# Dealing TensorE's turns anew: fewer visits for value products, levels among the last query slices

## What is computed

```python
def nsa_mixer(h, ...):                      # 16 heads of 64, 4 key/value groups
    q, kc, vc, ks, vs, kw, vw, gl, z = split_cols(h @ w_in, ...)
    q = rope(q); gates = sigmoid(gl)
    v_cmp = compress(vc, pe_v, wv1, wv2)    # silu(flat @ w1) @ w2 over blocks of 32 tokens
    k_cmp = rope(compress(kc, pe_k, wk1, wk2), cmp_end)
    o_c = masked_softmax(q . k_cmp) . v_cmp
    o_s = masked_softmax(q . rope(ks) at the selected blocks) . vs
    o_w = masked_softmax(q . rope(kw) in the window) . vw
    o = gates[0] * o_c + gates[1] * o_s + gates[2] * o_w
    return (o * silu(z)) @ w_out

def hgrn2_mixer(h, ...):                    # 8 heads of 128, chunks of 64
    q_raw, f_raw, i_in, z = split_cols(h @ w_in, ...)
    f = lb + (1 - lb) * sigmoid(f_raw); k = 1 - f; q = silu(q_raw)
    # o[t] = sum over s <= t of (q[t] * k[s] * product of f between) . v[s]
    o = o * rsqrt(mean(o * o) + EPS) * g_norm
    return (o * silu(z)) @ w_out
```

## Time and profile before

| | |
|---|---|
| median of 3 runs | 328.72 us (328.6 to 329.0) |
| profiled execution, first to last instruction (span) | 327.3 us |
| around the span (median less span) | 1.4 us |
| TensorE, matmuls | 316.1 us, 97% |
| TensorE, weight loads beside them | 268.5 us, 82% |
| VectorE | 228.5 us, 70% |
| ScalarE | 188.5 us, 58% |
| GpSimd | 56.8 us, 17% |
| from HBM | 47.97 MB |

### The profile page before, as it was taken

One profiled execution on the slowest core, in us unless ns is written; L12 is line 12 of the kernel. 1 busy time (PEld: TensorE's weight loads), 2 busy tenths in 40 slices (PEclk: granted clock), 3 DMA queues, 4 the chain that ended last, 5 costly groups with the idle time before them and its releaser, 6 DMA issues.

```text
span 327.3 us, 6178 instructions
## 1 busy us (share of the span) xinstructions
PE 316.1 (97%) x2380; PEld 268.5 (82%) x2380; DVE 228.5 (70%) x408; ACT 188.5 (58%) x400; POOL 56.8 (17%) x55
## 2 busy tenths in 40 slices
PE   8999999998999999999999999999999999998993
PEld 5789778867889887777678878999998788897882
DVE  2788953649659978979838716378359988489824
ACT  4694355347686676758545806838355027898223
POOL 0004022070343333446300000100000011111000
PEclk9999999999999999999999999999999999999998
DMA  7999999806390830043260783663663334002011
GB/s 234 393 326 215 272 358 198 258 36 210 97 209 1 194 67 2 0 131 128 75 248 0 259 299 95 240 228 92 212 241 110 150 112 151 3 0 66 0 64 64
DMA packets 28828, 49.41 MB, mean 151 GB/s; under 512 B 3256, under 2 KB 7744, under 8 KB 28800
## 3 DMA queue, kind: packets, MB, share of 16 engines
q1 hardware_dynamic: 25760, 44.30, 43.3%
q10 hardware_dynamic: 2528, 2.69, 4.1%
q0 software_dynamic: 512, 2.03, 1.9%
HBM read 47.97 MB, written 1.05 MB: 150 GB/s over the span
## 4 chain that ended last, share of the span: by engine, by line
PE 63%; DVE 16%; ACT 8%; issue 2%; POOL 2%; ACTq 0%; DVEq 0%; POOLq 0%
PE bank L553 58%; DVE w_lo L1079 6%; ACT w_hi L832 4%; PE bank L732 3%; POOL rp L1442 1%; DVE nmax L1283 1%; ACT prob L952 1%; PE bank L653 1%; DVE qk L1372 1%; DVE ft L1339 1%; DVE qk L1358 1%; DVE prob_t L1295 1%; PE bank L597 1%; DVE zT L1225 1%; DVE zT L1226 0%
## 5 line engine op out<-in xcount | busy, mean ns | idle before, releaser
L1079 DVE TENSOR_TENSOR w_lo<-raw,w_hi 128x1024 fp32r<-128x1024 f32 (+1 forms) x80 | 89.0, 1155 | 34.5 <-ACT w_hi L832 34.3
L553 PE MATMUL bank<-w_hi,h_hi 128*128 128x512 f32 x192 | 77.4, 409 | 2.0 <-DVE h_lo L1182 1.1
L553 PE MATMUL bank<-w_hi,h_lo 128*128 128x512 f32 x192 | 75.1, 391 | 0.0
L553 PE MATMUL bank<-w_lo,h_hi 128*128 128x512 f32 x192 | 75.1, 391 | 0.0
L832 ACT ACTIVATE w_hi<-raw 128x1024 fp32r<-128x1024 f32 (+1 forms) x80 | 72.9, 967 | 2.1 <-issue 1.9
L553 PE MATMUL bank<-h_hi,w_hi 128*128 128x256 f32 x224 | 64.9, 290 | 0.3 <-DVE vc_lo L1261 0.3
L553 PE MATMUL bank<-h_hi,w_lo 128*128 128x256 f32 x224 | 63.4, 283 | 0.0
L553 PE MATMUL bank<-h_lo,w_hi 128*128 128x256 f32 x224 | 63.3, 283 | 0.0
L553 PEld LDWEIGHTS bank<-w_hi,h_hi 128*128 128x128 f32 x192 | 35.9, 188 | 10.6 <-issue 3.7
L553 PEld LDWEIGHTS bank<-h_hi,w_hi 128*128 128x128 f32 x224 | 42.9, 192 | 1.1 <-DVE vc_lo L1261 0.7
L553 PEld LDWEIGHTS bank<-h_lo,w_hi 128*128 128x128 f32 x224 | 42.9, 192 | 0.2
(11 more groups left out here) (199 smaller groups left out, 424.0 us busy)
## 6 DMA issues: line engine op xcount, KB each, us to landing
raw<-in_hg SPq DMA_DIRECT2D x16, 1024.0 KB, 7.4
raw<-in_nsa SPq DMA_DIRECT2D x12, 1024.0 KB, 8.8
raw<-in_nsa_out SPq DMA_DIRECT2D x8, 512.0 KB, 8.5
raw<-in_hg_out SPq DMA_DIRECT2D x4, 1024.0 KB, 6.6
raw<-in_nsa SPq DMA_DIRECT2D x8, 256.0 KB, 5.7
w<-in_w1k SPq DMA_DIRECT2D x2, 1024.0 KB, 16.1
w<-in_w1v ACTq DMA_DIRECT2D x2, 1024.0 KB, 14.6
x_res<-in_x SPq DMA_DIRECT2D x4, 256.0 KB, 5.1
```

What stands on the lines that cost most here:

```text
L553: return nc.tensor.matmul(o, lhsT, rhs, start=start, stop=stop, skip_group_check=True)
L1079: m = V.tensor_tensor(lo, src, hi.bitcast(F32), ALU.subtract)
```

## The change

It replaces the two strings, and with them the numbers that place the splits: SPREAD, GATED_LAG (3 to 4) and LAG. Both strings hold the same letters as before, so that TensorE has the same steps and banks. In ORDER, two H come ahead of the first A. The first x (cmp1 of the keys) stands behind one E and no longer behind four. The g of a roped tile often stand in pairs. The v come in 9 groups and no longer in 13, the groups mixed anew with s, z and t. In H_ORDER, the transposes h and the first V slices change places by one. Three l stand ahead of the last two R. After the last levels the order is z o x o z x z z z z y y, where it was z o z z o z x z x y y, so that o(0,1) comes two slices of z earlier. The four r (V_O0, t1) stand in one run behind the first s, where r and s were mixed to the end.

```diff
--- before.py
+++ after.py
@@ -74,9 +74,9 @@
 LAST_LV = len(LEVELS)
 RECT_LV = (LAST_LV - 2, LAST_LV - 1)
 
-ORDER = 'HAHHBAHHBAHHBABCDCCrCDgDDgEEEEggxFFFGkFIIgJgkKKIgIgKKpxLggpkgppqqkgqzsgqzzgszzgatgzsbsszzztstszzvtcszvvvtstsszvtztsvtzastzsvvttsbstvvvtsosovvcotstssvvttssvttsotvtvvovttovvvvoo'
+ORDER = 'HHHAHHBAAHHBABBCDCrCCggDDggDExEEEFkFFFGgkKIKJggIKIIKxLgqpggppkpqkggqzsgqzgzszgaztgzsbsszzztstzszstvczvvvtsttzssvvatsszztsztvvttsbstvvvvtosstocostssvvsttsvvttsottvvvvottovvvvoo'
 HT_BANKS = ((4, 5, 6, 7), (0, 1, 4, 5))
-H_ORDER = 'aaaabhhbbbcccchdhddeeeefdfFffFFFFFFQFQQQQQQQGGGGGGRRGGRRRRRRllllzzllllzllllzzllllzzllllzllllzllllzzllllzozzozxzxyyoommmmnyynnnrssrsrrs'
+H_ORDER = 'aaaabhbhbbcccchhddeeeeffdfFdfFFFFFFQFQQQQQQQGGGRGGGGGRRRRRlRRlllzzllllzllllzzllllzzllllzllllzllllzlzlllzoxozxzzzyyoommmmnyynnnsrrrrsss'
 CMP_BANKS = ((1, 1, 7), (7, 6, 1))
 ACT_TURNS = (4, 7, 10, 11, 12, 13, 16, 19, 22)
 
@@ -214,11 +214,11 @@
     return kk + 1 if u == 0 else KT + NQ * (u - 1) + kk // 2 + 1
 
 
-SPREAD = {U_KW: (6, 7, 7, 0), U_Q0: (9, 5, 18, 15), U_Q1: (10, 13, 20, 26), U_Z0: (4, 0, 7, 12), U_Z1: (6, 7, 8, 12), U_O0: (17, 14, 28, 45), U_O1: (31, 47, 66, 93), V_V0: (0, 0, 1, 4), V_V1: (0, 0, 3, 6), V_F0: (0, 0, 11, 0), V_Q0: (2, 7, 20, 19), V_F1: (3, 5, 5, 6), V_Q1: (1, 0, 4, 9), V_Z0: (3, 5, 3, 5), V_Z1: (4, 0, 44, 39), V_O0: (0, 3, 2, 2), V_O1: (3, 1, 7, 4)}
-GATED_LAG = 3
+SPREAD = {U_KW: (10, 7, 7, 6), U_Q0: (1, 7, 20, 15), U_Q1: (1, 12, 5, 21), U_Z0: (5, 3, 2, 13), U_Z1: (3, 5, 11, 12), U_O0: (19, 0, 25, 38), U_O1: (31, 57, 78, 96), V_V0: (0, 0, 0, 4), V_V1: (0, 0, 2, 10), V_F0: (2, 0, 8, 0), V_Q0: (2, 0, 23, 25), V_F1: (0, 4, 1, 2), V_Q1: (2, 2, 10, 12), V_Z0: (0, 3, 0, 3), V_Z1: (0, 9, 56, 26), V_O0: (0, 3, 0, 0), V_O1: (0, 3, 7, 6)}
+GATED_LAG = 4
 CMP_LAG = 4
 GATED_AT = [max(LAST[("pv", job)], LAST[Z_GROUPS[-1]] + job) for job in range(4)]
-LAG = {U_O0: 2, U_O1: 3, V_Z0: 1, U_Z0: 1, U_Q1: 1, V_O1: 2, V_Q0: 3, V_F1: 2, V_Z1: 1, V_F0: 2, V_V1: 4, U_Z1: 2, U_KW: 2, U_Q0: 2, V_V0: 1, V_O0: 1, V_Q1: 2}
+LAG = {U_O0: 4, U_O1: 4, V_Z0: 2, U_Z0: 3, U_Q1: 2, V_O1: 2, V_Q0: 3, V_F1: 4, V_Z1: 1, V_F0: 5, V_V1: 4, U_Z1: 2, U_KW: 1, U_Q0: 1, V_V0: 1, V_O0: 4, V_Q1: 2}
 SPLIT_HI_AT, SPLIT_LO_AT = split_places()
```

## The result

| | before | after |
|---|---|---|
| median of the runs | 328.86 us (4 runs: 328.60, 328.72, 329.00 and 619.23) | 333.99 us (332.66 to 335.36, 4 runs) |
| ratio, 95% interval | 1 | 1.0153 (1.0130 to 1.0176) |
| profiled execution, span | 327.3 us | 330.9 us (its time 332.66) |
| mean granted clock of TensorE | 0.996 | 0.984 |

The change makes the kernel slower by 1.5%. Nothing on record explains the one execution of 619.23; without it the median of before is 328.72. The forecast was 329.2 us and its range ended at 331.3. The median is 5.1 us over that of before; the profiled execution is the quickest of the four and accounts for 3.6 of them.

A forecast was written before the change was run, and what follows sets the result against it. TensorE, busy 316.1 of 327.3 us, was taken as the bound. 3.15 - 1.0 - 0.35 + 0 - 1.25 - 0.1 = +0.45 gave span 327.7, with 1.4 around it 329.2 us; range 327.0 to 331.3.

The forecast's parts named there:

- Part 1: Head up to cmp1(0): moved ahead of three E slices, it waits some 5 us for w1k; +3.7 us.
- B: Rival at w1k's load: it lands earlier, at 37.7, making the time 326.8 us; chance 0.20.
- C: Rival at w1k's load: at 389 GB/s it lands at about 31, before TensorE comes; 324.0 us, chance 0.05.
- Part 2: From cmp1(0) to Z0's first slice: three old waits go, -1.8; a new stage 4 bank wait comes, +1.25 us.
- Part 3: Attention: fewer value-product visits -1.07, small pt waits gone -0.45, one new wait for prob_t +0.5; together -1.0 us.
- Rival A: VectorE and ScalarE fall behind in attention, pv visits wait: attention +0.5 instead of -1.0, time 331; chance 0.20.
- Part 4: Second layer's projections and levels: hT pair moved one turn, -0.35 us; the levels taken as 0.
- Part 5: End of HGRN2: o(0,1) earlier, so V_O0's first slice no longer waits for h_lo; -1.25 us.
- 6: Tail: VectorE's last add still starts right with the last matmul; -0.1 us.

The follow-up runs named there:

- filler: Changed kernel with 20 matmuls into an unused bank before the wait for w1k, results unread: 330.64 us, ratio 1.0052.
- second profile: The changed kernel run once more, unaltered, for the spread of its executions: 333.11 us, ratio 1.0138, span 333.6.
- w1k_rows: Changed kernel with w1k in another arrangement, 16 KB pieces instead of 1 KB, still two transfers to 64 partitions each: 331.69 us.
- w1k_2x128: Changed kernel with w1k rearranged as two 1 MB transfers, each to all 128 partitions in 8 KB pieces: 325.92 us, ratio 0.9903.
- w1k_128: Changed kernel with w1k rearranged as one transfer of 16 KB to each of 128 partitions: 326.00 us, ratio 0.9911.
- w1_two: Changed kernel with the second half of w1k issued from ScalarE's queue at about 20.5 us: 331.08 us, ratio 1.0070.
- w1_j: Changed kernel with w1k cut by j into 16 transfers of 128 KB, each to all 128 partitions: 364.39 us, ratio 1.1083.
- att_only: Kernel before with only the new order from Z0's first slice to attention's end, its splits and GATED_LAG 4: 328.69 us, ratio 0.9988.
- h_only: Kernel before with only H_ORDER and layer 1's split places from the changed kernel: 328.09 us, ratio 0.9973.
- best3: Changed kernel, cmp1(0) behind four E slices, cmpT(0) and Q0's first splits moved too, before's late-query-and-level order and V_Z0/V_Z1 splits: 325.56 us, ratio 0.9889.
- filler_10: Changed kernel with 10 unread matmuls, not 20, before the wait for w1k: two runs, 330.28 and 336.20 us.

## Why the prediction was wrong, point by point

**Part 1 (cmp1(0), forecast +3.7).** The mechanism, its place and the landing were right: start forecast at 40.1 and measured at 39.73, idle "some 5 us" and measured 4.7, due to w1k. The step that failed is its price: "0.4 earlier, with 4.1 undone" leaves out what the idle time does to the work behind it. cmp1(0) took 5.69 for 3.60, +2.1, and run filler takes just that away (3.60 again, and 1.9 less of span with a start 0.3 later). The trace before had the clock at 1.00 up to 40.5 us, and TensorE's longest wait in it was 1.2 us; a forecast that makes a wait of 5 us must not take the clock from such a trace. The Trainium skill has it ("TensorE: Matmul & The Clock Gate", HAM oscillation): an array that waits long enough for a DMA drops to the half clock and pays for it behind the wait. The traces agree: 3.60 against 5.69 and 6.33 us for one and the same step. The prediction had no such rival and should have had it as the chief one.

By the same step the spread was missed. In the earlier trace rows the landing of w1k had little in front of it, and the one profile of before could not show whether it moves. The second profile of the changed kernel has it 2.2 us later, with 6.33 us at the low clock. As far as these two profiles show, this alone parts the profiled 332.66 from longer executions.

**Rivals B and C (w1k earlier).** Both fell: the landing was at 39.59. For C I had weighed a rule on the size of the pieces against the earlier trace rows and left open what the 194 GB/s are. w1k_rows and w1k_2x128 settle it: from 1 KB up the pieces didn't matter, the 64 partitions did. The Trainium skill says it ("SBUF — State Buffer", Door 1: The DMA port swizzle, and Can I just issue two DMAs to hit both halves?): partitions 0 to 63 lie on half of the ports, two transfers to the two halves serialize, and only one transfer over all 128 partitions reaches every port. w1k_128 (379 for 195 GB/s) agrees with the first and the last of these; what it says of two transfers no run here shows, as in w1_two the halves were hardly under way together. And w1_j agrees with the Trainium skill's "DMA: Bandwidth & Descriptors", Why a DMA increments its semaphore by 16 and not by 1: the number of engines divides the slowest dimension of both sides, which leaves 2 here; the DMA share of 0.14 is that of some two. C's price was near in its sign and within 2.0 us: it put 324.0, and a w1k that lands early gives 326.0.

**Part 2 (-1.8 and +1.25).** From the end of cmp1(0) to Z0's first slice the changed kernel gains 0.64 (5.38 behind, three slices counted, to 4.74), where -0.55 was forecast. That the sum comes so close is luck: the wait for hid is gone as forecast, but the new wait at stage 4 is 0.4 by the record, not 1.25. A wait for hidT (0.3) is new and 0.2 of the wait ahead of Z0 is left; some 0.2 to 0.3 I have not followed.

**Part 3 (attention, -1.0).** The wait was sized about right at 0.5, but it comes twice: 0.7 and 0.45. With the gain by visits taken as forecast (it was not measured by itself), -1.07 - 0.45 + 1.15 = -0.4, and att_only measured -0.32. What failed is the count "would wait 0.5 once". The earlier trace rows showed VectorE with hardly any slack; each visit that takes the product of a transpose just made should have been priced. Rival A (+0.5) fell as well.

**Part 4 (levels, 0).** The hT turns gave -0.38 as forecast. The levels were +0.97. h_only and best3 put it on this stretch of the order and the split places that go with it; by the starts in the two traces it is +0.8 by the three levels ahead of the last two V_Q1 slices (a passage more, and a wait for silu of q, forecast at 0.1 to 0.4 and then "set against the levels themselves"), then -1.0 and +0.8 as waits for VectorE's qk updates go and come, and +0.4 for one more passage at the last level. The step that failed is taking 0 for a stage with several terms of a microsecond each.

**Part 5 (-1.25) and 6 (-0.1).** -1.39 and 0. Right: h_lo is no longer waited for at V_O0, which follows the last cross product by one pitch:

```profile
302.09 0.39 PE L553 MATMUL bank<-v_hg,attx 128*128 128x128 f32 x2
302.24 0.48 PE L553 MATMUL bank<-w_hi,h_hi 128*128 128x512 f32 x1
```

**The sum.** Forecast +0.45 on the span. With the clock's 2.1, attention's 0.7 and the levels' 1.0 it would be +4.2; cmp1(0)'s landing (0.4) and parts 2 and 5 (0.1 each) came out better, which leaves the 3.6 of the profile. The median is 1.3 to 1.5 above that; a later landing of w1k, as in the second profile, would do it, but the executions in the middle have no profile.

## What to carry to other kernels

Where an edit brings a wait of some microseconds in front of TensorE, price the work behind it at the low clock too, and expect the executions to spread with the landing; if the wait can't be avoided, matmuls that nobody reads are worth their time. Load SBUF tiles with transfers that write all 128 partitions and whose slowest dimension divides into many, before any thought on the size of pieces of 1 KB and more. In a kernel whose splits and evictions are placed by step number, a step can't be moved alone: follow what each in-order queue then holds ahead of what TensorE waits for.

## What the runs showed of the hardware that I had not expected

- TensorE's granted clock fell to 0.50 after idle times of 2.9 us (w1_two) and more and stayed at 1.00 after 1.9 us (filler_10) and the kernel's other waits of about 1 us. It fell some 2.5 us into the wait in one profile of the changed kernel and some 5 us into it in the other. After it cmp1(0) took 5.3 to 6.4 us for 3.6.
- Two loads of 1 MB to 64 partitions each ran at 191 to 201 GB/s at a DMA share of about 1, with pieces of 1 KB or 16 KB; the same bytes to 128 partitions ran at 379 to 387.
- Transfers whose source has a slowest dimension of 2 ran at 47 GB/s, at a DMA share of 0.14 (w1_j).
- The last of w1k's landings came 1.1 and 3.6 us after all the others (39.59 and 41.75 in two profiles of one kernel), and that one landing set when cmp1(0) started.
